# Two matmul records per product instead of three, in the feed-forward blocks that have 256 tokens

## The reference

```
def swiglu(h, w_in, w_out):                       # w_in 1024 x 5632, w_out 2816 x 1024
    gate, up = jnp.split(h @ w_in, 2, axis=-1)
    ...                                           # silu(gate) * up, then @ w_out

h = h + 0.5 * swiglu(rms_norm(h, g[2]), ffn_w_in[i, 1], ffn_w_out[i, 1])
return h[:, N_META:]                              # 16 meta tokens are dropped: 256 are left

hn = rms_norm_2(h, norm_ffn_g)                    # second block
hid = jnp.square(jax.nn.relu(jnp.einsum('bsd,df->bsf', hn, w_ff1)))   # 1024 -> 4096
h = h + jnp.einsum('bsf,fd->bsd', hid, w_ff2)                         # 4096 -> 1024
```

## Time and profile before

| | |
|---|---|
| median of 3 runs | 1580.85 us (1578.48 to 1580.94) |
| the profiled execution, whole | 1576.64 us |
| its span | 1574.8 us |
| mean granted TensorE clock | 0.992 of full speed |
| PE busy | 1535.1 us, 97% |
| PE weight load busy | 1473.5 us, 94% |
| POOL busy | 1136.0 us, 72% |
| ACT busy | 780.5 us, 50% |
| DVE busy | 659.8 us, 42% |

### The profile page before, as it was taken

How to read it: one execution, slowest core, us unless ns; L and a number is a source line. 1 busy time by engine, 2 the same in 40 slices (tenths; PEclk the granted TensorE clock), 3 DMA queues, 4 the chain that set the end, 5 groups by cost and what they waited for, 6 DMA issues and landing times.

```text
span 1574.8 us, 40654 instructions
## 1 busy us (share of the span) xinstructions
PE 1535.1 (97%) x16113; PEld 1473.5 (94%) x16113; DVE 659.8 (42%) x1608; ACT 780.5 (50%) x1289; POOL 1136.0 (72%) x848
## 2 busy tenths in 40 slices
PE   6999999999899999999999999999999999999998
PEld 6999999888899999999999998699999988899998
DVE  4334568764546333223332248653352436442200
ACT  5444557632345444455444444754445545565532
POOL 6876857983538877778787785088878985478885
PEclk9999999999899999999999999999999999999999
DMA  7544543310023544465444642065545543245552
GB/s 271 187 164 151 167 164 134 107 69 2 2 83 108 187 181 140 166 206 186 162 161 150 210 159 75 2 230 209 182 135 187 204 141 123 93 147 181 182 187 78
DMA packets 37908, 231.30 MB, mean 147 GB/s; under 512 B 4527, under 2 KB 6680, under 8 KB 16552
## 3 DMA queue, kind: packets, MB, share of 16 engines
q1 hardware_dynamic: 36552, 228.57, 41.5%
q10 hardware_dynamic: 1248, 1.24, 0.2%
HBM read 228.67 MB, written 2.63 MB: 147 GB/s over the span
## 4 chain that ended last, share of the span: by engine, by line
PE 74%; DVE 2%; issue 1%; ACT 1%; POOL 0%; DVEq 0%; POOLq 0%; ACTq 0%
PE PS L842 60%; PE PS L841 1%; PE PS L1101 1%; PE PS L1108 1%; PE PS L1116 1%; PE PS L1522 1%; PE PS L1146 1%; PE PS L1140 1%; PE PS L1298 0%; PE PS L1290 0%; PE PS L1091 0%; PE PS L1508 0%; PE PS L1498 0%; POOL wlo L796 0%; PE PS L1127 0%
## 5 line engine op out<-in xcount | busy, mean ns | idle before, releaser
L796 POOL TENSOR_TENSOR wlo<-raw,whi 128x256 fp32r<-128x256 f32 (+1 forms) x742 | 1068.8, 1470 | 344.8 <-ACT whi L2784 322.9
L842 PE MATMUL PS<-xh,whi 128*128 128x272 f32 (+1 forms) x2304 | 666.4, 289 | 20.3 <-POOL wlo L796 15.8
L842 PE MATMUL PS<-xl,whi 128*128 128x272 f32 (+1 forms) x2304 | 658.1, 286 | 0.0
L842 PE MATMUL PS<-xh,wlo 128*128 128x272 f32 (+1 forms) x2304 | 657.4, 285 | 0.0
L2784 ACT ACTIVATE whi<-raw 128x1024 fp32r<-128x1024 f32 x468 | 455.6, 982 | 358.7 <-PE PS L842 338.7
L842 PEld LDWEIGHTS PS<-xh,whi 128*128 128x128 f32 x2304 | 433.8, 188 | 29.2 <-issue 21.9
L842 PEld LDWEIGHTS PS<-xl,whi 128*128 128x128 f32 x2304 | 435.1, 189 | 0.6
L842 PEld LDWEIGHTS PS<-xh,wlo 128*128 128x128 f32 x2304 | 435.6, 189 | 0.0
L842 PE MATMUL PS<-hid_h,whi 128*128 128x272 f32 (+1 forms) x960 | 273.8, 285 | 2.1 <-POOL wlo L796 2.1
L842 PE MATMUL PS<-hid_h,wlo 128*128 128x272 f32 (+1 forms) x960 | 273.8, 285 | 0.0
L842 PE MATMUL PS<-hid_l,whi 128*128 128x272 f32 (+1 forms) x960 | 272.9, 284 | 0.0
(11 more groups left out here) (436 smaller groups left out, 1624.0 us busy)
## 6 DMA issues: line engine op xcount, KB each, us to landing
raw<-w_f_in_in SPq DMA_DIRECT2D x88, 1024.0 KB, 4.8
raw<-w_f_dn_in SPq DMA_DIRECT2D x64, 704.0 KB, 4.1
raw<-w_b_ff_in SPq DMA_DIRECT2D x32, 1024.0 KB, 4.8
raw<-w_rk_k_in SPq DMA_DIRECT2D x4, 1024.0 KB, 4.9
raw<-w_rk_r_in SPq DMA_DIRECT2D x4, 1024.0 KB, 4.8
raw<-w_rk_v_in SPq DMA_DIRECT2D x4, 1024.0 KB, 5.3
raw<-w_rk_o_in SPq DMA_DIRECT2D x4, 1024.0 KB, 5.4
raw<-w_at_q_in SPq DMA_DIRECT2D x4, 1024.0 KB, 5.2
```

Source lines behind the costliest of these rows:

```text
L796: last = nc.gpsimd.tensor_tensor(wlo[U % SPL][:, piece], raw[U % RAW][:, piece], whi[U % SPL][:, piece].bitcast(F32), ALU.subtract)
L842: mm(out, a, b, start=start and n == 0, stop=stop and n == 2, **kw)
```

## The change

For the 256-token blocks the high and low parts of an input lie in one tile (`xs0`, `hid`, `hid2`), high first. `two_sums` multiplies the high weight by both in one matmul record of 512 columns, into the two halves of one PSUM bank, and adds low weight times high input to the first half in a record of 256. The bank then holds two sums; whoever drains it adds the second half to the first: `low_sum` copies the second half to SBUF (`outt`, free at that time) and adds it (in f3_in once a half, in b_ff1 once a unit, over both banks); f3_dn and b_ff2 have one more add into h for each output chunk. The last output chunk of b_ff2 keeps the three records. The blocks of 272 tokens are left as they are, since 544 columns don't fit a bank.

```diff
-        xh[0] = xr("xh0", [128, KC, T], F32R)
-        xl[0] = xr("xl0", [128, KC, T], F32R)
+        xs0 = xr("xs0", [128, 2, KC, T], F32R)
+        xh[0], xl[0] = xs0[:, 0, :, :], xs0[:, 1, :, :]
...
-        hid_h = ff("hid_h", [128, FC * T], F32R)
-        hid_l = ff("hid_l", [128, FC * T], F32R)
+        hid = ff("hid", [128, 2, FC * T], F32R)
+        hid_h, hid_l = hid[:, 0, :], hid[:, 1, :]
...
+            def two_sums(bank_, w, x, start, stop):
+
+                both = PS[:, bank_, 0:2 * SEQ].rearrange("p (s n) -> p s n", n=SEQ)
+                high = PS[:, bank_, 0:SEQ]
+                if start:
+                    mm(both, w[0], x, start=True, stop=False, skip_group_check=True)
+                    return mm(high, w[1], x[:, 0, :], start=False, stop=stop, skip_group_check=True)
+                mm(high, w[1], x[:, 0, :], start=False, stop=stop, skip_group_check=True)
+                return mm(both, w[0], x, start=False, stop=stop, skip_group_check=True)
...
+                                if n == SEQ:
+                                    last = two_sums(bank(G) + mi, weights(U, ALLR, slice(c, c + 128)), xs0[:, :, k, 0:n],
+                                                    k == 0, k == KC - 1)
+                                else:
...
+                                o = slice(kk * stride, kk * stride + n)
+                                if n == SEQ and not (name == "b_ff2" and m == 7):
+                                    last = two_sums(bank(G), weights(U, ALLR, slice(k * 128, k * 128 + 128)), hid_[:, :, o],
+                                                    kk == 0, kk == nk - 1)
+                                else:
...
-                turns(link, 8, 2, 0, body, 2)
+                if name == "b_ff2":
+                    body(range(2), None)
+                    with link.loop(2, 0) as i:
+                        body(range(2, 4), i)
+                    body(range(6, 8), None)
+                else:
+                    turns(link, 8, 2, 0, body, 2)
...
+            def low_sum(total, part, between):
+                step(v.tensor_copy(between, part))
+                step(v.tensor_tensor(total, total, between, ALU.add))
...
                     dve.wait_ge(s_unit, val(2 * U + 1, i, 8))
+                    if n == SEQ:
+                        low_sum(PS[:, bank(G), 0:n], PS[:, bank(G), n:2 * n], outt[:, 0, :])
...
                     dve.wait_ge(s_unit, val(2 * U + 2, i, 8))
+                    if n == SEQ:
+                        low_sum(PS[:, bank(G) + 1, 0:n], PS[:, bank(G) + 1, n:2 * n], outt[:, 1, :])
...
+                    if name == "f3_dn":
+                        step(v.scalar_tensor_tensor(x, PS[:, bank(G) + q, n:2 * n], factor, x, ALU.mult, ALU.add))
                     ins = v.scalar_tensor_tensor(x, src, factor, x, ALU.mult, ALU.add)
...
                     dve.wait_ge(s_unit, val(2 * (U + 1), i, 8))
+                    low_sum(PS[:, bank(G):bank(G) + 2, 0:SEQ], PS[:, bank(G):bank(G) + 2, SEQ:2 * SEQ], outt[:, 0:2, :])
...
                 dve.wait_ge(s_unit, 2 * (U + 1))
+                if m < 7:
+                    step(v.tensor_tensor(hv(SEQ, m)[:, 0, :], PS[:, bank(G), SEQ:2 * SEQ], hv(SEQ, m)[:, 0, :], ALU.add))
```

More of the change, by code:

```diff
@@ L308, in build @@
         ff = Region(after_x0)
-        hid2_h = ff("hid2_h", [128, 32 * SEQ], F32R)
-        hid2_l = ff("hid2_l", [128, 32 * SEQ], F32R)
+        hid2 = ff("hid2", [128, 2, 32 * SEQ], F32R)
+        hid2_h, hid2_l = hid2[:, 0, :], hid2[:, 1, :]
         act2 = ff("act2", [128, 2, 2, SEQ])
@@ L907, in body @@
                                 c = mi * 1024 + k * 128
-                                last = products(PS[:, bank(G) + mi, 0:n], weights(U, ALLR, slice(c, c + 128)),
-                                                (xh[b][:, k, 0:n], xl[b][:, k, 0:n]), k == 0, k == KC - 1)
+                                if n == SEQ:
+                                    last = two_sums(bank(G) + mi, weights(U, ALLR, slice(c, c + 128)), xs0[:, :, k, 0:n],
+                                                    k == 0, k == KC - 1)
+                                else:
+                                    last = products(PS[:, bank(G) + mi, 0:n], weights(U, ALLR, slice(c, c + 128)),
+                                                    (xh[b][:, k, 0:n], xl[b][:, k, 0:n]), k == 0, k == KC - 1)
                                 if u == 0 and mi == 0 and squared is not None:
@@ L926, in project, with project_down @@
                     turns(link, UN[name], 4, 0, body)
-            def project_down(name, n, hh, hl, stride, nk, ready):
+            def project_down(name, n, hid_, stride, nk, ready):
                 half = nk // 2
@@ L944, in body @@
                                     ready(kk)
-                                last = products(PS[:, bank(G), 0:n], weights(U, ALLR, slice(k * 128, k * 128 + 128)),
-                                                (hh[:, kk * stride:kk * stride + n], hl[:, kk * stride:kk * stride + n]),
-                                                kk == 0, kk == nk - 1)
+                                o = slice(kk * stride, kk * stride + n)
[3 more added lines that the diff above has]
+                                else:
+                                    last = products(PS[:, bank(G), 0:n], weights(U, ALLR, slice(k * 128, k * 128 + 128)),
+                                                    (hid_[:, 0, o], hid_[:, 1, o]), kk == 0, kk == nk - 1)
                                 if k in (7, half - 1):
                                     last.then_inc(s_unit, 1)
-                turns(link, 8, 2, 0, body, 2)
+                if name == "b_ff2":
[5 more added lines that the diff above has]
+                    turns(link, 8, 2, 0, body, 2)
             def swiglu(f):
@@ L958, in swiglu @@
                     mm(PS[0:8, bank(G) + 1, 0:384], relb[:, :], distt[:, :], start=True, stop=True).then_inc(s_bwm, 1)
-                project_down(f + "_dn", tok[f], hid_h, hid_l, T, FC,
+                project_down(f + "_dn", tok[f], hid, T, FC,
                              lambda kk: pe.wait_ge(s_hlo, HB[f] + kk + 1))
@@ L1873, in _ @@
             project("b_ff1", SEQ, 0, "ff", norm="ff", straight=4, squared=squares, drained=G0["b_o"] + 4)
-            project_down("b_ff2", SEQ, hid2_h, hid2_l, SEQ, 32,
+            project_down("b_ff2", SEQ, hid2, SEQ, 32,
                          lambda kk: pe.wait_ge(s_hlo2, kk // 2 + 1))
@@ L1968, in body @@
                             third(u - 2, i)
-                turns(step, FC, 4, 4, body, 6)
+                turns(step, FC, 4, 20 if n == SEQ else 4, body, 6)
                 second(FC - 1, None)
@@ L2039, in residual @@
                     return
-                turns(step, 8, per, 0, body, 1)
+                turns(step, 8, per, per if name == "f3_dn" else 0, body, 1)
                 after_act(7, None)
@@ L2768, in _ @@
             ff1(range(4), None)
-            with step.loop(3, 0) as i:
+            with step.loop(3, 8) as i:
                 ff1(range(4, 8), i)
```

## The result

| | before | after |
|---|---|---|
| median (14 runs each, on the same chip) | 1580.38 us (1573.06 to 1582.56) | 1584.63 us (1578.08 to 1590.01) |
| ratio | | 1.0033, 95% interval 1.002 to 1.0047 |
| span of the profiled execution | 1574.8 us | 1586.1 us |
| mean granted clock of it | 0.992 | 0.987 |

The forecast was 1573.0 us, faster. The kernel became slower by 4 to 5 us. The slower rival had been priced at 1584.5 us; it held 10 chances in 100.

What follows compares the result with a forecast made beforehand. PE was taken to bound the kernel, by columns plus 11.9 ns a record. Gain 12.0 - 0.1 less costs 1.87 + 0.58 + 1.6 = 4.05 gave 7.85 us less, 1573.0 us; own range 1570.5 to 1576, overall 1562 to 1579.

Steps and rivals of the forecast that it cites:

- slower rival: No gain, stalls only: each source run costs 11.9 ns, the long record 237.2 ns; 1584.5 us; chance 10%.
- The gain: f3_in, f3_dn, b_ff1, b_ff2: one record fewer saves 11.9 ns in each of 1008 products, 12.0 us.
- Drains in the steady stages: f3_in, b_ff1, b_ff2: added copies and adds stay covered and cost nothing; uncovered, f3_in would lose up to 19 us.
- First place: f3_dn, third chunk: POOL 1.34 us later, PE 0.52 us sooner, so PE's stall grows by 1.87 us to 3.7.
- Second place: f3_dn to the next block: one more add with its step on the path, 0.58 us, bounds 0.4 to 0.7.
- Third: Behind the longer f3_dn stall the clock likely drops to half for 3.4 us, costing 1.6 us, between 0 and 1.7.
- All this costs nothing while covered: Added drain work in f3_in, b_ff1 and b_ff2 hides behind PE; f3_in's weights are needed 8.2 us later.

Runs made afterwards that it cites:

- m2_pairs: Own program, PE alone at the kernel's operand addresses, products of three records against two: 356.7 and 355.7 ns in f3_in, 355.0 and 353.3 in b_ff2.
- run 512: Not a follow-up run: the words "in one run 512 columns" mean source columns lying together, a record of 227.1 ns in m1_records.
- m1_records: Own program, long rows of equal records on PE, alone and beside other engines: 256 columns 117.5 ns, 512 columns 227.1 in one run, 231.7 in two.
- e_drains: Changed kernel with three records of 256 columns a product again, all added drains kept: 1584.5 us, 1.0021 of the kernel before.
- e_f3_only: Kernel before with only f3_in and f3_dn changed, with their drains: 1583.85 us, 1.0025.
- e_angles_before: Kernel before with the second half of the angles moved behind the first drain of f3_dn: 1577.68 us, 0.9986.
- e_rows_angles: Kernel before (three records) with weights at 64 of 128 bytes, 256-token inputs in 1024-byte rows, angles' second half behind f3_dn's first drain: 1576.32 us, 0.9976.
- e_align_after: Changed kernel with the weights 32 bytes lower: 1580.27 us, 0.9995 of the kernel before.
- e_ff_only: Kernel before with only b_ff1 and b_ff2 changed, with their drains: 1577.13 us, 0.9986, no measurable change.
- e_rows_after: Changed kernel with angles' second half behind f3_dn's first drain, weights and inputs at 64 of 128 bytes, 1024-byte rows: 1574.5 us, 0.9979 of the kernel before.
- e_align_before: Kernel before with the weights 32 bytes lower, inputs unmoved: 1582.91 us, 1.0022.
- e_rows_before: Kernel before with weights at 64 of 128 bytes and 256-token inputs in rows of 1024 bytes: 1576.05 us, 0.998.

## Why the prediction was wrong

- **The gain, which failed.** The step was: both forms have 11.9 to 12.0 ns on top, "a fixed part comes with each record", hence 225.2 ns for 512 columns and 12.0 us for 1008 products. In place of it: at f3_in's places 512 columns take 232.7 ns alone and 236 to 238 alternating with the short record (`m2_pairs` and the kernel), 19 to 25 ns above their columns. 1.3 us were saved. At one place and in one run 512 columns have only 13.8 ns on top (`m1_records`), close to the forecast; the two widths of the earlier trace rows couldn't tell that the part moves with the places and with the neighbour. PE alone shows it, at the kernel's byte places and with no other engine at work, so POOL, DVE, transfers, the shared bank and the change of weight buffer are excluded as the cause. What inside PE's reading of weights and input makes it is open.
- **A row was missed.** The text says that no float32r record of 512 columns is in the trace. There are twelve, in the attention of the second block. PE's timeline of the kernel before:

```profile
1292.04 0.40 PE L841 MATMUL PS<-whi,lath 128*128 128x512 f32 x1
1292.27 0.39 PE L841 MATMUL PS<-whi,latl 128*128 128x512 f32 x1
1292.51 0.40 PE L841 MATMUL PS<-wlo,lath 128*128 128x512 f32 x1
1292.74 0.39 PE L841 MATMUL PS<-whi,lath 128*128 128x512 f32 x1
```

  0.70 us for three, 233 ns each, in one run (here the weights stream, 512 columns, and the input stands still). That is the very figure from which the slower rival "decides". With it the gain would have been 4 us by 1008 x (355.8 - 233.3 - 118.6), and the sum no change at most.
- **The slower rival** had the time (1584.5) and the product (unchanged) nearly right and the mechanism wrong: it isn't the two runs, which cost 4.6 ns at one place (`m1_records`) and nothing at another (`m2_pairs`, 232.7 against 233.2 in one run). That its time fits to 0.1 us is luck: it had no gain and 3.6 us of costs, where the runs show 1.3 and 4.6.
- **Drains in the steady stages:** right. Copy 0.42 us (forecast 0.39), adds 0.43 (0.42), 512 wide 0.69 and 0.70 (0.71 and 0.69); POOL waits and stays at its 2.4 us; no wait of PE.
- **First place,** the stall in f3_dn: +1.7 against +1.87. PE came hardly sooner (0.2 us, 44 products at 4.6 ns, not 0.52), and the chain over DVE, ACT and POOL grew by 1.5 us where 1.34 was put: two misses that cancel in part.
- **Second place:** 0.46 against 0.58, within its bounds. **Third,** the clock: 3.4 us at half clock right behind the stall, 1.5 us, against 1.6. The price of 1.7 for such a stretch is a little high, since a product takes 0.64 us there, no more than its 768 columns at 1.2 GHz, as the prediction says itself.
- **"All this costs nothing while covered":** true in the steady units, false for the first one. There the drain waits for the reciprocal, and the cover of 8.2 us is used up before; 0.9 us of `low_sum` became a stall of about 1 us.

Costs in all 4.6 us against 4.05 forecast; gain 1.3 against 12.0. What isn't settled is the further stretch at half clock in the attention, 2.4 us in the profile of after: it is also in those of `e_drains` and `e_f3_only`, which have the long stall, but at about that place in those of `e_angles_before` and `e_rows_angles` too, which have no stall in f3_dn, and not in that of `e_align_after`, which has the long one.

## What to carry to other kernels

Time over count of one record form is the price of that form in that sequence of operand places; don't split it into columns and a fixed part and carry the part to another width. Search the trace for the new form first (here twelve records by form would have answered it), and if it isn't there, run the new record and its neighbour by themselves at the kernel's own addresses: PE alone gave the kernel's 356 ns to within 1 ns. When work is added to a drain, look at the first unit of the stage and at the stage behind it, where the cover is thin; the loss was there, and moving unrelated work out of that gap took some 8 us off the changed kernel, where the change had been forecast to save 7.85.

## What was unexpected of the hardware

- A record's time beyond its columns moves with the byte places of its weights and input: 256 columns of rounded float32 113.5 to 119.9 ns; a product of three such records 340.2 to 356.8 ns with the same work.
- The spacings repeat exactly: in f3_in every fourth long record or so holds the next one up for 0.256 us where the others do for 0.228 to 0.238, in the kernel and with PE alone.
- The data don't matter (`m1_records`: with zeros as input, read at one place, 120.0 ns at 256 columns, as with data read at one place; 227.0 at 512), nor do four other kinds of traffic.
- At half clock the part above the columns is gone: a product of 768 columns takes 0.64 us behind the stall, which is 768 columns at 1.2 GHz.
- After a stall of about 2 us the clock can go either way: at the start of b_ff1, always 2.1 to 2.2 us from record to record, half clock followed in seven of the twelve profiles (before, after, `e_ff_only`, `e_f3_only`, `e_align_after`, `e_rows_angles`, `e_rows_after`) and not in the other five. Behind 1.9 to 2.0 us in f3_dn it stayed at full in all four that had them (before, `e_ff_only`, `e_align_before`, `e_rows_before`), and behind 3.4 us and more there it fell in all four (after, `e_drains`, `e_f3_only`, `e_align_after`), for 3.4 us in three of them and for 6.8 us in `e_align_after`. What sets it isn't known from these runs.
